# Forgetting attention in a hybrid layer: scores of two heads at a time from the two halves of TensorE's rows

## The reference

```
q, k = rmsnorm(q), rmsnorm(k)                  # per head, 64 features
c = cumsum(log_sigmoid(f_raw + fgate_b))       # per head, over the tokens
for each block of 128 queries:
    scores = q @ k.T / 8 + c[query] - c[key]
    probs  = softmax(where(key <= query, scores, -inf))
    out    = probs @ v
```

## Time and profile before

| | |
|---|---|
| median of three runs | 2748.56 us |
| the profiled execution | 2746.44 us |
| its span | 2744.5 us |
| TensorE busy in the span | 2688.0 us |
| VectorE, ScalarE, GpSimd busy | 1168.4, 1022.7, 221.1 us |
| granted TensorE clock, mean | 0.998 of full speed |

### The profile page before, as it was taken

How to read it: one execution, slowest core, us unless ns; L and a number is a source line. 1 busy time by engine, 2 the same in 40 slices (tenths; PEclk the granted TensorE clock), 3 DMA queues, 4 the chain that set the end, 5 groups by cost and what they waited for, 6 DMA issues and landing times.

```text
span 2744.5 us, 41129 instructions
## 1 busy us (share of the span) xinstructions
PE 2688.0 (98%) x15562; PEld 2140.8 (78%) x15562; DVE 1168.4 (43%) x1717; ACT 1022.7 (37%) x1460; POOL 221.1 (8%) x348
## 2 busy tenths in 40 slices
PE   8999999999999999999999999999999999999998
PEld 6776776776777688888888888888888888888787
DVE  6654653663663535333333333333333333334543
ACT  5435534534644424433223332233332222234421
POOL 3001210210111103000000000000000000011300
PEclk9999999999999999999999999999999999999999
DMA  4221231231132432322233222332223322223332
GB/s 168 87 76 58 69 94 59 70 86 56 65 91 90 133 98 98 107 99 94 87 95 107 99 93 85 98 107 99 92 88 95 108 98 93 95 86 108 106 119 76
DMA packets 108136, 255.91 MB, mean 93 GB/s; under 512 B 35288, under 2 KB 37848, under 8 KB 108024
## 3 DMA queue, kind: packets, MB, share of 16 engines
q1 hardware_dynamic: 105920, 247.10, 28.3%
q0 software_dynamic: 2112, 7.34, 0.8%
HBM read 245.43 MB, written 8.98 MB: 93 GB/s over the span
## 4 chain that ended last, share of the span: by engine, by line
PE 72%; issue 18%; POOL 3%; DVE 3%; ACT 2%; DMA 1%; SPq 1%; POOLq 0%; DVEq 0%; ACTq 0%
PE bank L318 23%; PE bank L315 23%; PE bank L319 23%; PE bank L356 1%; POOL probs L1097 1%; POOL scratch_pool L129 1%; DVE w_lo L310 1%; DMA raw<-w_mix 1%; ACT w_hi L303 0%; POOL sg_t L1089 0%; SPq L1305 0%; PE bank L481 0%; POOL carried L1124 0%; POOL M_t L1111 0%; PE bank L510 0%
## 5 line engine op out<-in xcount | busy, mean ns | idle before, releaser
L310 DVE TENSOR_TENSOR w_lo<-raw,w_hi 128x1024 fp32r<-128x1024 f32 (+1 forms) x484 | 546.1, 1130 | 965.2 <-ACT w_hi L303 964.5
L303 ACT ACTIVATE w_hi<-raw 128x1024 fp32r<-128x1024 f32 (+1 forms) x484 | 471.7, 975 | 963.2 <-PE bank L319 940.4
L315 PE MATMUL bank<-hn_hi,w_hi 128*128 128x512 f32 x1664 | 648.1, 389 | 0.0
L319 PE MATMUL bank<-hn_hi,w_lo 128*128 128x512 f32 x1664 | 647.3, 389 | 0.0
L318 PE MATMUL bank<-hn_lo,w_hi 128*128 128x512 f32 x1664 | 647.3, 389 | 0.0
L315 PE MATMUL bank<-in_hi,w_hi 128*128 128x512 f32 x1088 | 455.9, 419 | 29.9 <-DVE in_lo L1689 11.6
L318 PE MATMUL bank<-in_lo,w_hi 128*128 128x512 f32 x1088 | 441.7, 406 | 0.0
L319 PE MATMUL bank<-in_hi,w_lo 128*128 128x512 f32 x1088 | 428.0, 393 | 0.0
L318 PEld LDWEIGHTS bank<-hn_lo,w_hi 128*128 128x128 f32 x1664 | 312.3, 188 | 65.5 <-issue 0.5
L315 PEld LDWEIGHTS bank<-hn_hi,w_hi 128*128 128x128 f32 x1664 | 312.3, 188 | 65.2 <-issue 0.5
L319 PEld LDWEIGHTS bank<-hn_hi,w_lo 128*128 128x128 f32 x1664 | 312.3, 188 | 64.8
(11 more groups left out here) (240 smaller groups left out, 2123.3 us busy)
## 6 DMA issues: line engine op xcount, KB each, us to landing
raw<-w_gu SPq DMA_DIRECT2D x176, 512.0 KB, 3.4
raw<-w_mix SPq DMA_DIRECT2D x116, 512.0 KB, 3.6
raw<-w_down SPq DMA_DIRECT2D x64, 384.0 KB, 3.1
raw<-w_down SPq DMA_DIRECT2D x64, 320.0 KB, 2.9
raw<-ple_gate SPq DMA_DIRECT2D x32, 512.0 KB, 3.4
raw<-w_mix SPq DMA_DIRECT2D x28, 384.0 KB, 3.2
h_t<-xT SPq DMA_DIRECT2D x4, 1024.0 KB, 6.2
out<-h_t POOLq DMA_DIRECT2D x16, 256.0 KB, 2.3
```

Of the source, the lines that this page charges most:

```text
L303: nc.scalar.activation(w_hi[:, ring_slots(par2, half), 0:cols[half]], raw[:, half, 0:cols[half]], ACT.Copy).then_inc(hi_ready, 1)
L310: nc.vector.tensor_tensor(w_lo[:, s, 0:cols[half]], raw[:, half, 0:cols[half]], w_hi[:, s, 0:cols[half]].bitcast(F32), ALU.subtract).then_ ...
L315: nc.tensor.matmul(out, w_h, x_hi, start=start, stop=False, skip_group_check=True)
L319: return nc.tensor.matmul(out, w_l, x_hi, start=False, stop=stop, skip_group_check=True)
```

## The change

The scores of two heads (items 2 m and 2 m + 1) are computed in one step, every ten steps: one head from partitions 0 to 63, the other from partitions 64 to 127, each into its own PSUM bank. Their masks are four products of 64 rows. c[query] is dropped. -c[key] comes as a tile `c_keys` that one DMA broadcasts to all 128 partitions (1 MB per group), and VectorE adds it to the scores while it moves them from PSUM to `probs`; the maximum and the exponential then read `probs`. Items are numbered so that two heads alternate: item q is head 2 (q // 8) + q % 2, query block (q // 2) % 4. q and k are written by one VectorE operation per pair of heads.

```diff
-    q_aug = sb("q_aug", [P, GH, SEQ])
-    k_aug = sb("k_aug", [P, GH, SEQ])
+    q_t = sb("q_t", [P, 2, SEQ])
+    k_t = sb("k_t", [P, 2, SEQ])
+    c_keys = sb("c_keys", [P, GH, SEQ])
...
     def pe_attention(pe, s, kt, gp):
         q = attention_item(s, kt, "scores")
-        if q is not None:
-            j, i = q // TT, q % TT
+        if q is not None and q % 2 == 0:
+            pair, i = q // (2 * TT), q // 2 % TT
             if q == 0:
-
                 pe.wait_ge(S("fox_qk_ready"), 4 * gp + 4)
-                pe.wait_ge(S("c_rows_landed"), 32 * (gp + 1))
-            if q >= 2:
-                pe.wait_ge(S("probs_ready"), 16 * gp + q - 1)
+            else:
+                pe.wait_ge(S("scores_biased"), 16 * gp + q)
             n = (i + 1) * P
-            bank = s_bank[q % 2]
-            nc.tensor.matmul(bank[:, 0:n], q_aug[0:HD + 2, j, tok(i)], k_aug[0:HD + 2, j, 0:n],
-                             start=True, stop=False, skip_group_check=True)
-
-            nc.tensor.matmul(bank[:, tok(i)], id16[:, 0:P], id16[:, P:2 * P],
-                             start=False, stop=True, skip_group_check=True).then_inc(S("scores_done"), 1)
+            for h in range(2):
+                nc.tensor.matmul(s_bank[h][:, 0:n], q_t[hp(h), pair, tok(i)], k_t[hp(h), pair, 0:n],
+                                 start=True, stop=False, skip_group_check=True)
+            for part in range(2):
+                for h in range(2):
+                    ins = nc.tensor.matmul(s_bank[h][:, tok(i)], id16[hp(h), tok(part)], id16[hp(h), tok(2 + part)],
+                                           start=False, stop=part == 1, skip_group_check=True)
+                    if part == 1:
+                        ins.then_inc(S("scores_done"), 1)
...
     def act_attention(act, s, kt, gp):
...
-            n = (q % TT + 1) * P
+            n = (q // 2 % TT + 1) * P
             act.wait_ge(S("max_ready"), 16 * gp + q + 1)
-            if q >= 2:
-
-                act.wait_ge(S("probs_turned"), 16 * gp + q - 1)
-            nc.scalar.activation(probs[:, q % 2, 0:n], s_bank[q % 2][:, 0:n], ACT.Exp,
+            nc.scalar.activation(probs[:, q % 2, 0:n], probs[:, q % 2, 0:n], ACT.Exp,
...
     def dve_attention(dve, s, kt, gp):
         q = attention_item(s, kt, "scores")
         if q is not None:
+            n = (q // 2 % TT + 1) * P
+            if q == 0:
+                dve.wait_ge(S("c_keys_landed"), 16 * (gp + 1))
             dve.wait_ge(S("scores_done"), 16 * gp + q + 1)
-            nc.vector.tensor_reduce(small[:, 8 + q % 2:9 + q % 2], s_bank[q % 2][:, 0:(q % TT + 1) * P], AX.X,
+            if q >= 2:
+
+                dve.wait_ge(S("probs_turned"), 16 * gp + q - 1)
+            nc.vector.tensor_tensor(probs[:, q % 2, 0:n], s_bank[q % 2][:, 0:n],
+                                    c_keys[:, 2 * (q // (2 * TT)) + q % 2, 0:n], ALU.add
+                                    ).then_inc(S("scores_biased"), 1)
+            dve.wait_ge(S("scores_biased"), 16 * gp + q + 1)
+            nc.vector.tensor_reduce(small[:, 8 + q % 2:9 + q % 2], probs[:, q % 2, 0:n], AX.X,
                                     ALU.max, negate=True).then_inc(S("max_ready"), 1)
...
-            dst, gain = (q_aug, qg8) if c < 2 else (k_aug, gain_of("k_g"))
-            for hh in range(2):
-                ps = slice(HD * hh, HD * hh + HD)
-                ins = nc.vector.scalar_tensor_tensor(out=dst[0:HD, 2 * (c % 2) + hh, :], in0=u_t[ps, 1:SEQ + 1],
-                                                     scalar=gain[ps, :], in1=t2[ps, :], op0=ALU.mult, op1=ALU.mult)
-            ins.then_inc(S("fox_qk_ready"), 1)
+            dst, gain = (q_t, qg8[:]) if c < 2 else (k_t, gain_of("k_g"))
+            nc.vector.scalar_tensor_tensor(out=dst[:, c % 2, :], in0=u_t[:, 1:SEQ + 1], scalar=gain, in1=t2[:],
+                                           op0=ALU.mult, op1=ALU.mult).then_inc(S("fox_qk_ready"), 1)
...
-                        sp.dma_start(q_aug[HD + 1:HD + 2, :, :], c_dram[0:1, cg, :]).then_inc(S("c_rows_landed"), 16)
-                        sp.dma_start(k_aug[HD:HD + 1, :, :], c_dram[1:2, cg, :]).then_inc(S("c_rows_landed"), 16)
+                        sp.dma_start(c_keys[:], c_dram[cg, :].partition_broadcast(P)).then_inc(S("c_keys_landed"), 16)
```

More of the change, by code:

```diff
@@ L134, in layer @@
     y_dram = f32("y_scratch", [KT, P, SEQ]).ap()
-    c_dram = f32("c_scratch", [2, 16, SEQ]).ap()
+    c_dram = f32("c_scratch", [16, SEQ]).ap()
     blocks_dram = f32("blocks_scratch", [P // SB, SB, SB, SB]).ap()
@@ L254, in layer @@
     consts = sb("consts", [P, C_COL + 8])
-    id16 = sb("id16", [P, 2 * P], BF16)
+    id16 = sb("id16", [P, 4 * P], BF16)
     g_par = sb("g_par", [P, 2, NG_PAR])
@@ L470, in pe_attention @@
         q = attention_item(s, kt, "scores")
-        if q is not None:
-            j, i = q // TT, q % TT
+        if q is not None and q % 2 == 0:
+            pair, i = q // (2 * TT), q // 2 % TT
             if q == 0:
                 pe.wait_ge(S("fox_qk_ready"), 4 * gp + 4)
-                pe.wait_ge(S("c_rows_landed"), 32 * (gp + 1))
-            if q >= 2:
-                pe.wait_ge(S("probs_ready"), 16 * gp + q - 1)
+            else:
+                pe.wait_ge(S("scores_biased"), 16 * gp + q)
             n = (i + 1) * P
-            bank = s_bank[q % 2]
-            nc.tensor.matmul(bank[:, 0:n], q_aug[0:HD + 2, j, tok(i)], k_aug[0:HD + 2, j, 0:n],
-                             start=True, stop=False, skip_group_check=True)
-            nc.tensor.matmul(bank[:, tok(i)], id16[:, 0:P], id16[:, P:2 * P],
-                             start=False, stop=True, skip_group_check=True).then_inc(S("scores_done"), 1)
+            for h in range(2):
[7 more added lines that the diff above has]
+                        ins.then_inc(S("scores_done"), 1)
         q = attention_item(s, kt, "turn")
         if q is not None:
-            i = q % TT
+            i = q // 2 % TT
             pe.wait_ge(S("probs_normed"), 16 * gp + q + 1)
@@ L764, in act_attention @@
         if q is not None:
-            j, i = q // TT, q % TT
+            i = q // 2 % TT
             n = (i + 1) * P
             act.wait_ge(S("probs_turned"), 16 * gp + q + 1)
-            if i == 0 and j == 2:
-                act.wait_ge(S("pv_done"), 4 * gp + j)
-            nc.scalar.activation(probs_T[j % 2][:, 0:i + 1, tok(i)],
+            if q == 2 * TT:
+                act.wait_ge(S("pv_done"), 4 * gp + 2)
+            nc.scalar.activation(probs_T[q % 2][:, 0:i + 1, tok(i)],
                                  pt_bank[q % 2][:, 0:n].rearrange("p (k c) -> p k c", c=P), ACT.Copy
@@ L1105, in pool_clear @@
         if c == NC // 2:
-            pool.wait_ge(S("c_stored"), 32)
+            pool.wait_ge(S("c_stored"), 16)
             if not (isinstance(g, int) and g == 0):
@@ L1287, in _ @@
             sp.wait_ge(S("c_ready"), 1)
-            for i in range(2):
-                sp.dma_start(c_dram[i], cf[LORA:LORA + 16, i, :]).then_inc(S("c_stored"), 16)
+            sp.dma_start(c_dram, cf[LORA:LORA + 16, 1, :]).then_inc(S("c_stored"), 16)
             def store_rwkv(gp):
@@ L1339, in group @@
                         sp.dma_start(g2_t[:], d["g2"][g]).then_inc(S("g2_landed"), 16)
-                        sp.wait_ge(S("c_stored"), 32)
-                        sp.wait_ge(S("aug_ones_ready"), 2)
+                        sp.wait_ge(S("c_stored"), 16)
                         cg = bass.ds(GH * g, GH) if gp is not None else slice(0, GH)
-                        sp.dma_start(q_aug[HD + 1:HD + 2, :, :], c_dram[0:1, cg, :]).then_inc(S("c_rows_landed"), 16)
-                        sp.dma_start(k_aug[HD:HD + 1, :, :], c_dram[1:2, cg, :]).then_inc(S("c_rows_landed"), 16)
+                        sp.dma_start(c_keys[:], c_dram[cg, :].partition_broadcast(P)).then_inc(S("c_keys_landed"), 16)
                     if s == 7:
@@ L1713, in _ @@
             dve_arrival_lora(dve, 2)
-            dve.wait_ge(S("aug_ones_ready"), 2)
             dve.wait_ge(S("u_column_cleared"), 1)
@@ L1910, in _ @@
             pool.wait_ge(S("u_column_cleared"), 1)
[L1911 to L1914, removed]
             pool.wait_ge(S("consts_landed"), 32)
@@ L2042 @@
     import ml_dtypes
-    id16 = np.concatenate([(i == j).astype(np.float32), np.where(j > i, np.float32(-1e30), np.float32(0))], 1
-                          ).astype(ml_dtypes.bfloat16)
+    halves = lambda m: np.concatenate([np.concatenate([m[:HD], m[HD:]], 1)] * 2)
+    id16 = np.concatenate([halves((i == j).astype(np.float32)),
+                           halves(np.where(j > i, np.float32(-1e30), np.float32(0)))], 1).astype(ml_dtypes.bfloat16)
     arrays = {
```

## The result

The changed kernel takes 2758.4 us (median of 6 runs, 2754.4 to 2762.4); the kernel before, run beside it, 2747.95 (6 runs, 2746.4 to 2748.8). The ratio is 1.004, 95% interval 1.003 to 1.005: slower by 0.4%. The forecast was 2750.7, so 7.7 us are missing in it; the time lies above its own range (2747 to 2754) and within that of the rivals (to 2760), and it rose by more than the 5.5 us that the forecast took for no change. The profiled execution took 2754.43 us with a span of 2752.8; against the one before (2746.44, 2744.5) it is 8.3 longer in the span.

A forecast was written before the change was run, and what follows sets the result against it. TensorE, busy 2688.0 of 2744.5 us, was taken to bound the kernel, with the other engines' chain setting stretches of attention. Three groups +2.7, tail -0.6: +2.1 on 2748.56 gives 2750.7 us, range 2747 to 2754.

The forecast's parts named there:

- the rivals: VectorE's chain 2756.7 (0.20), no overlap 2757.6 (0.07), slow broadcast 2758 (0.06), TensorE gains more 2743.5 (0.15); ends 2743 to 2760.
- Row halves side by side: TensorE's scores: the two heads' halves overlap fully, so scores take 2.16 us per pair of heads.
- Entering and leaving the shape, 0.42 us a pair: TensorE, each step of two heads' scores: changing array shape costs 0.42 us, ends 0 and 0.6, leaving 4.2 us gained.
- First half, +0.6: Each group, items 0 to 6 up to L363 in slab 2: TensorE's L363 comes 0.6 us later, after waiting 1.2.
- Second half, +0.3: Each group, item 10 to item 15's transposes: earlier table loads offset VectorE's added work, leaving +0.3 us with hand-overs.
- the 0.5 that the forecast gave as a sign of being wrong: Item 15's transposes more than 0.5 us earlier or later against the group's item 10 would show the forecast wrong.
- the forecast's rival of VectorE's chain: Second half does not shorten because another wait holds the table loads: 2.9 us per group, 2756.7; chance 0.20.
- VT_t: Slabs 7 to 10: one VectorE operation instead of two for q and k saves 0.2 us at best.
- VectorE's additional work: VectorE's sum of busy time, whole kernel: up by 30 - 12 = 18 us.
- Broadcast free: c_keys DMA of 1 MB per group: lands in 6.2 us, before the store of the solved blocks, costing nothing.
- The tail, -0.6: After the groups: waits for L1750 0.4 us longer, TensorE gains 1.0 from item 2 on; together -0.6.

The follow-up runs named there:

- the two kernels above: Kernel before with only the new order, two heads a step: 2754.4 us; changed kernel without VectorE's add and with its subtractions late: 2742.1 us.
- The copy in the kernel before: Kernel before, with VectorE also copying each item's scores from PSUM to probs ahead of the maximum: 2761.8 us, ratio 1.005.
- the moved product: VectorE's receptance-decay product issued behind low_of_t, besides late subtractions: 2742.2 us on the changed kernel, 2737.2 on the kernel before.
- the executions listed above: The changed kernel's twelve executions by mean granted clock, from 2754.4 us at 0.998 to 2765.6 at 0.993; kernel before, median 2748.3 at 0.998.
- the changed kernel's second trace: Trace from running the changed kernel once more, unaltered, beside the kernel before: 2762.7 us, ratio 1.0049.
- the best version: Kernel before, with VectorE's two subtractions of weights issued behind low_of_t in slab 5: 2737.6 us, ratio 0.9961.

## Why the forecast fell short

**Row halves side by side: right.** 0.75 us for two heads 384 wide.

**Entering and leaving the shape, 0.42 us a pair: too dear.** By the rows of 276.72 to 278.19, a plain product is followed by the pair after 0.31 instead of 0.23, the scores take 0.75 where 0.65 would be the content, the masks 0.21 for 0.11, and two transposes 0.20 for 0.14. That is 0.34, and the tail of the two kernels above makes it 0.28 (0.42 less 1.0 us in seven steps). With 0.3 for 0.42, TensorE gains 4.2 + 32 x 0.12 = 8 us, not 4.2. It made no difference to the forecast: except in the tail TensorE stands waiting where the gain falls due.

**First half, +0.6: right.** 0.68, 0.55 and 0.67 in the three groups at L364, counted from the product behind the VT_t wait before it, with a wait of 1.32 for the 1.2 forecast.

**Second half, +0.3: the step that failed.** From the product with v (now at 302.73) to item 15's transposes the groups take 1.33, 1.32 and 1.31 longer, over the 0.5 that the forecast gave as a sign of being wrong. The forecast let ScalarE's table loads come 0.8 and 1.6 earlier, since the copies ahead of them wait less. ScalarE in order of time, after:
```profile
315.99 0.28 ACT L769 ACTIVATE probs_T_odd<-bank 128x128 f32<-128x128 f32 x1 [0.81 <-PE bank L499]
317.30 1.28 ACT L681 ACT_TABLE_LOAD   x1 [1.03 <-POOL sg_t L1095]
...
326.59 1.28 ACT L692 ACT_TABLE_LOAD   x1
328.09 0.63 ACT L692 ACTIVATE t<-t 128x512 f32<-128x512 f32 x1 [0.22 <-DVE t L912]
```
The first load did come off the copy, but it stands behind the wait of its own activation for GpSimd's L1095, which ends at 317.20, and starts at 317.30, 0.48 later than in the earlier trace rows. GpSimd's operation is 0.6 late because the exp of item 10 is 0.68 late: the pair's scores end later than the single one did, and the add stands before the maximum. The second load starts at 326.59, 0.79 earlier than before (327.38), where 1.6 was forecast; it ran without waiting for the sum, but the sum arrives 0.22 after it, and item 13's exp, now wider, follows. Of the 1.4 that were to reach L918, now L917, 0.44 did (331.47, before 331.91). From there to the reciprocal of item 15 VectorE has not one idle moment:
```profile
331.47 0.75 DVE L917 SCALAR_TENSOR_TENSOR t<-t,g_par,t 128x512 f32<-128x512 f32 x1
...
334.52 0.68 DVE L1003 TENSOR_TENSOR probs<-bank,c_keys 128x512 f32<-128x512 f32 x1
335.24 0.69 DVE L1007 TENSOR_REDUCE small<-probs 128x1 f32<-128x512 f32 x1
...
339.25 0.68 DVE L1003 TENSOR_TENSOR probs<-bank,c_keys 128x512 f32<-128x512 f32 x1
339.96 0.69 DVE L1007 TENSOR_REDUCE small<-probs 128x1 f32<-128x512 f32 x1
...
342.74 0.16 DVE L1012 RECIPROCAL small<-small 128x1 f32<-128x1 f32 x1
```
11.27 us against 9.49 before (341.40 - 331.91): +1.78, of which two adds and a wider maximum are 1.56 from start to start, and two operations that run beside GpSimd's scaling 0.2 (L925, 0.87 for 0.77, and L822, 0.79 for 0.69); less 0.44. This is the forecast's rival of VectorE's chain, for the first load with the mechanism it named (another wait holds it). The copy in the kernel before and the moved product show VectorE to be the chain. That the rival's 2756.7 is near the median is in part luck: it had 2.9 us a group where 2.2 were measured without the clock, and no clock.

**No price for TensorE's clock: a second failure.** In groups 2 and 3 the wait, now 3.3 us, brought the clock to its lower level, 1.4 us each in the profiled execution and more in others. With the wait shortened to 1 us the clock stayed up there, and the median came down by 4.5 us more than the waits. At an equal clock the change costs some 6 us where the forecast had 2.1, so VectorE's chain and the clock each make about 4 of the missing us.

**Sum by the profiled executions:** groups 9.4 instead of 2.7, of which the clock is 2.8; without it 2.2 a group, where the forecast had 0.9. The other 2.2 us up to +10.5 between the medians go with the clock by the executions listed above: the changed kernel's second trace is 9.3 us longer than its first with nearly the same waits, and the clock falls in five places instead of two.

**VT_t.** In group 1 L966's saving and TensorE's idle time before the sum in slab 9 gave 0.5 back (387.39 against 386.54, from +1.34 to +0.85), and the VT_t wait took it again (1.81 for 1.38): +1.31 behind it. No lasting saving, as forecast.

**VectorE's additional work: right.** 18.3 us for the 18 forecast; only where it falls was priced too low.

**Broadcast free: right.** Landed in 5.0 us, before the solved blocks are stored; without the add it was issued all the same, in a kernel faster than before.

**The tail, -0.6: -0.3.** Its waits grew by 0.4 as forecast.

## What to carry to other kernels

Of an operation added to an engine that is 43% busy, ask what it costs in the stretch in which that engine does not idle: here 18 us of work on VectorE cost 10 to 12 us of time at an equal clock and 14 to 18 in the medians. Before letting a table load or a copy move forward, look for every semaphore that the instruction behind it waits for, not only the one that ended its wait last. And read the wait on the critical path for what stands beside its work on other engines: the best version came not from doing less but from moving two subtractions of a few microseconds' slack out of GpSimd's way.

## What the runs showed of the hardware

GpSimd beside VectorE. A scaling of 128x512 in SBUF took 2.19 us beside VectorE's subtractions with two operands in SBUF, and 0.69 once they stood behind it; the scratch operation 1.09 and 0.19. The subtractions were as fast either way (2.34 and 2.35 for two). That is the lock of the Trainium skill (SBUF — State Buffer, "SBUF: two separate sides"): a VectorE operation that reads two SBUF operands and a GpSimd operation that reads SBUF exclude each other for the whole instruction, and do not share. The trace agrees for the scratch operation, which started behind the first subtraction and ended 0.09 us after it. The scaling, started behind the second, ended 1.1 after it and 0.5 after low_of_t, which reads two SBUF operands as well; whether low_of_t held it too isn't shown. With the subtractions late GpSimd's scaling is the first to start, and VectorE's low_of_t is the one that lasts longer, 1.03 for 0.69:
```profile
340.94 1.03 DVE L885 TENSOR_TENSOR low_of_t<-t,high_pair_of_bonus 128x512 fp32r<-128x512 f32 x1 [0.45 <-ACT high_pair_of_bonus L697]
```

VectorE's own scaling, with one operand in SBUF, was slowed too: 1.43 to 2.36 us beside GpSimd's clearing of M_t, which took 2.19 for 1.92 in the first case and 1.92 in the others, and 0.49 in the tail.

TensorE's clock. It fell behind every item 15 wait of 3.3 us or more in groups 2 and 3, though not in group 1 of the changed kernel, and in some executions behind waits of 1.6 to 2.5 us; in others it stayed at 1.00 behind waits just as long (2.57, without the add and with the subtractions late). Why it fell in one and not in the other isn't settled.
